# Norm stages of a two-layer encoder: a second unit's low halves placed after the scaling, spare matmuls, split transfers

## The chip, the cores and the metric

One NeuronCore of a Trainium2 chip runs the whole kernel in one launch. The metric is the device time of that core in microseconds (us), the median of several executions; lower is better.

## The reference

The kernel computes two layers of an encoder over 256 tokens of width 1024, all in float32.

```
x = x + mixer(rmsnorm(x, norm_mix[i]))     # layer 0: gated delta net, layer 1: Mamba-2 SSD
x = x + peer(rmsnorm(x, norm_ffn[i]))      # product-key expert retrieval over 128 x 128 experts
...
return rmsnorm(x, norm_final)
rmsnorm(x, w) = x * rsqrt(mean(x * x) + 1e-6) * w
```

Each of the four inner norms stands between two stages of heavy matrix products; a fifth norm makes the output. The change is in these norms, in the loading of x and in the storing of the output.

## The kernel before

**Weights.** All weight matrices come as a stream of *units* of 128x1024 floats (512 KB). SP (SyncE) loads them into `ring`, which has four slots. Every product of the stream is made of three products of rounded parts, hi x hi, lo x hi and hi x lo, so each unit is cut in two halves of 128x512 and each half is split: ScalarE writes the rounded part `w_hi` (L1368, signal `hi_ready`), then GpSimd (L1739) or, in the expert stages, VectorE (L900) writes the rest `w_lo = ring - w_hi` (signal `lo_ready`). Four halves fit in `w_hi` and `w_lo`. TensorE (L359) waits for `lo_ready` of the half it is about to use and raises `half_used`. SP reloads a ring slot when its low halves are made. ScalarE splits two units ahead.

**A norm.** `norm(i)`, i = 0 to 3, has a part on each engine. VectorE adds the products of the last stage to `x_sb` (L908, `x_added`), and ScalarE squares and sums four 128x512 pieces (L1394). VectorE makes the mean (L860), ScalarE its root (L1399), VectorE the factor (L862 to L867). Eight scalings of 128x256 on VectorE (L874) write `h_tok` (an area of `arena`), each raises `n_h`. TensorE's `turn_h` waits for two of them at a time and transposes four 128x128 blocks into a PSUM bank (L379), sixteen in all. ScalarE copies eight 128x256 pieces to `hT_hi` (L1368), VectorE writes the corrections to `hT_lo` (L878), and the first unit's products take them one by one (`await_h`). Each unit of these stages is 24 products of 256 columns into one bank, which ScalarE then copies out (L1368 `arena<-bank`).

**The units around a norm.** The first unit of the next stage is split before the norm. ScalarE splits the second one right after the root, in `norm(i)`, and GpSimd makes its low halves as soon as `hi_ready` allows, since `rest_of_units(..., at[...] + 2)` runs over both units. After the second unit GpSimd issues the load of the expert keys (norms 1 and 3, L1756), or splits the gate weights (norm 2, L1760 and L1762, behind waits for `n_h`, `half_used` and the gates' load).

**The ends.** SP loads x in one transfer of 1 MB (L317), then the first units. ScalarE issues the constants and the norm weights, GpSimd eleven small loads; GpSimd waits for all eleven before it splits the first gate weights and makes its first low half. The last norm multiplies two pieces of 128x1024 (L1361), and SP stores both in one transfer of 1 MB (L352). `Sqrt` on ScalarE needs a function table other than the one loaded first in norm 0; in the later norms a dummy `Sqrt` on `n_idle` loads it ahead of the squares.

**What sets the order.** Every engine's program is written out by hand, and only the named semaphores tie them together; there is no scheduler.

## Time and profile before

| | |
|---|---|
| median of 3 runs | 2238.69 us (2238.45 to 2240.41) |
| profiled execution | 2239.61 us |
| its span, first to last instruction | 2237.8 us |
| mean granted TensorE clock | 0.982 |
| TensorE matmul busy | 2149.9 us (96%) |
| VectorE, ScalarE, GpSimd busy | 1485.1, 1335.9, 1072.2 us |
| norm 0, 1, 2, 3, 4 in the span | 7 to 19, 276 to 290, 1124 to 1137, 1378 to 1392, 2226 to 2234 us |

The profile is of one execution and is read against that execution's own time. Busy TensorE is not TensorE at its peak, since the ends of matmuls are modelled. The granted clock is given as a share of the full 2.4 GHz; 0.5 is 1.2 GHz. A row of the timeline shows the start, the length, the engine, the line, the operation with its target and source, shapes and count, and in brackets how long the engine was idle before it and what released it.

### The profile page before, as it was taken

What the parts mean: (1) busy time and instruction counts of PE and PEld (TensorE: products, weight loads), DVE (VectorE), ACT (ScalarE), POOL (GpSimd) and SP (SyncE); (2) the same over time, 40 slices, a digit from 0 to 9 for tenths busy, and PEclk for the clock granted to TensorE, in tenths of its full rate; (3) what the DMA queues carried; (4) which work ended last, traced back from release to release, by engine and by line L of the source; (5) the groups of instructions that cost most, each with busy time, mean ns of one, the idle gap of its engine ahead of it and who ended that gap; (6) DMA issues with size and microseconds to landing.
All of it is one profiled execution on the core that took longest, in us unless ns stands there. A gap on an engine that the chain in (4) does not pass through costs nothing.

```text
span 2237.8 us, 46017 instructions
## 1 busy us (share of the span) xinstructions
PE 2149.9 (96%) x14384; PEld 1983.2 (89%) x14384; DVE 1485.1 (66%) x3206; ACT 1335.9 (60%) x2736; POOL 1072.2 (48%) x827
## 2 busy tenths in 40 slices
PE   7989799999999999999989988999999999999998
PEld 6979699999999988888889877999999999888886
DVE  5766319994666577777766662299666665777776
ACT  6754355578777644444466765555777885444444
POOL 6841377997766700000056447799976675000000
PEclk9989899999999999999999989999999999999999
DMA  5520254554444566666645225555544445666664
GB/s 169 166 61 1 65 168 146 169 170 158 141 141 140 157 196 193 193 194 190 196 123 161 86 76 169 158 173 161 177 144 138 140 141 173 194 195 190 196 190 148
DMA packets 93872, 343.66 MB, mean 154 GB/s; under 512 B 10688, under 2 KB 10752, under 8 KB 93152
## 3 DMA queue, kind: packets, MB, share of 16 engines
q1 hardware_dynamic: 92592, 338.21, 49.5%
q0 software_dynamic: 912, 4.07, 0.6%
q8 instruction: 47, 0.77, 0.1%
q10 hardware_dynamic: 288, 0.34, 0.0%
q14 instruction: 33, 0.27, 0.0%
HBM read 341.53 MB, written 1.05 MB: 153 GB/s over the span
## 4 chain that ended last, share of the span: by engine, by line
PE 82%; POOL 7%; issue 5%; DVE 3%; ACT 2%; DMA 0%; POOLq 0%; DVEq 0%; ACTq 0%
PE bank L359 80%; POOL w_lo L1739 7%; PE bank L524 0%; ACT w_hi L1368 0%; PE bank L379 0%; DMA small<-in_ssd_d 0%; ACT arena L1394 0%; DVE arena L874 0%; ACT arena L1368 0%; DVE arena L989 0%; DVE arena L1190 0%; DVE arena L1029 0%; DVE arena L996 0%; DVE arena L925 0%; ACT arena L1529 0%
## 5 line engine op out<-in xcount | busy, mean ns | idle before, releaser
L1739 POOL TENSOR_TENSOR w_lo<-ring,w_hi 128x512 fp32r<-128x512 f32 x744 | 994.1, 1350 | 682.9 <-ACT w_hi L1368 670.7
L1368 ACT ACTIVATE w_hi<-ring 128x512 fp32r<-128x512 f32 x1280 | 802.7, 628 | 530.3 <-PE bank L359 527.8
L359 PE MATMUL bank<-hT_hi,w_hi 128*128 128x256 f32 x2688 | 779.8, 290 | 7.9 <-POOL w_lo L1739 6.0
L359 PE MATMUL bank<-hT_lo,w_hi 128*128 128x256 f32 x2688 | 761.0, 283 | 0.0
L359 PE MATMUL bank<-hT_hi,w_lo 128*128 128x256 f32 x2688 | 760.9, 283 | 0.0
L359 PEld LDWEIGHTS bank<-hT_hi,w_hi 128*128 128x128 f32 x2688 | 515.8, 192 | 18.9 <-POOL w_lo L1739 18.4
L359 PEld LDWEIGHTS bank<-hT_lo,w_hi 128*128 128x128 f32 x2688 | 516.4, 192 | 0.0
L359 PEld LDWEIGHTS bank<-hT_hi,w_lo 128*128 128x128 f32 x2688 | 515.5, 192 | 0.0
L900 DVE TENSOR_TENSOR w_lo<-ring,w_hi 128x512 fp32r<-128x512 f32 x536 | 378.2, 706 | 197.3 <-ACT w_hi L1368 189.9
L359 PE MATMUL bank<-w_hi,p_ag_hi 128*128 128x512 f32 x1024 | 398.4, 389 | 0.0
L359 PE MATMUL bank<-w_lo,p_ag_hi 128*128 128x512 f32 x1024 | 398.4, 389 | 0.0
L359 PE MATMUL bank<-w_hi,p_ag_lo 128*128 128x512 f32 x1024 | 398.3, 389 | 0.0
L359 PEld LDWEIGHTS bank<-w_hi,p_ag_lo 128*128 128x128 f32 x1024 | 192.2, 188 | 40.1
L359 PEld LDWEIGHTS bank<-w_hi,p_ag_hi 128*128 128x128 f32 x1024 | 192.2, 188 | 40.0
L359 PEld LDWEIGHTS bank<-w_lo,p_ag_hi 128*128 128x128 f32 x1024 | 192.2, 188 | 39.6
L1283 DVE TENSOR_TENSOR arena<-bank,arena 128x512 f32 (+1 forms) x128 | 88.4, 691 | 166.9 <-PE bank L359 166.9
L359 PE MATMUL bank<-arena 128*128 128x128 f32 (+2 forms) x1072 | 138.0, 283 | 9.4 <-ACT arena L1543 3.2
L359 PEld LDWEIGHTS bank<-arena 128*128 128x128 f32 x1072 | 134.0, 198 | 13.5 <-issue 3.6
L925 DVE SCALAR_TENSOR_TENSOR arena<-bank,small,arena 128x254 f32<-128x254 f32 x192 | 92.5, 482 | 49.1 <-ACT arena L1368 43.7
L1676 ACT ACTIVATE work<-work,small 128x128 f32<-128x128 f32 x256 | 112.8, 488 | 20.2 <-ACT work L1670 19.6
L1326 DVE TENSOR_TENSOR p_ag_lo<-arena,p_ag_hi 128x256 fp32r<-128x256 f32 x256 | 111.0, 433 | 8.9
L1649 ACT ACTIVATE work<-bank 128x256 f32<-128x256 f32 x144 | 55.1, 383 | 84.4 <-PE bank L359 84.4
(241 smaller groups left out, 2244.5 us busy)
## 6 DMA issues: line engine op xcount, KB each, us to landing
ring<-in_peer_u SPq DMA_DIRECT2D x256, 512.0 KB, 3.5
ring<-in_peer_v SPq DMA_DIRECT2D x256, 512.0 KB, 4.1
ring<-in_peer_wq SPq DMA_DIRECT2D x32, 512.0 KB, 3.5
ring<-in_gdn_qkv SPq DMA_DIRECT2D x24, 512.0 KB, 3.5
ring<-in_ssd_xbc SPq DMA_DIRECT2D x24, 512.0 KB, 3.6
ring<-in_ssd_z SPq DMA_DIRECT2D x16, 512.0 KB, 3.5
ring<-in_ssd_out SPq DMA_DIRECT2D x16, 512.0 KB, 3.6
ring<-in_gdn_z SPq DMA_DIRECT2D x8, 512.0 KB, 3.5
```

The costliest lines, as they stand in the source:

```text
L359: return pe.matmul(o, w, r, start=first, stop=last)
L900: dve.tensor_tensor(w_part[1][:, s, :], ring[:, n % RING, hf * 512:(hf + 1) * 512], w_part[0][:, s, :].bitcast(F32), ALU.subtract).then_in ...
L925: ins = dve.scalar_tensor_tensor(o, bank[:, lo + s:hi + s], taps[:, m, j:j + 1], o, ALU.mult, ALU.add)
L1283: dve.tensor_tensor(v, PS[2 + q % 4][:, :].rearrange("p (t i) -> p i t", t=4), v, ALU.mult).then_inc(SEM["p_mul"], 1)
L1326: dve.tensor_tensor(p_ag[1][:, i % 2, :], v, p_ag[0][:, i % 2, :].bitcast(F32), ALU.subtract).then_inc(SEM["p_ag"], 1)
L1368: return act.activation(o, i, ACT.Copy, scale=scale)
L1649: act.activation(p_act[:, i % 2, :], PS[i % 2][:, 0:T], ACT.Gelu).then_inc(SEM["p_gelu"], 1)
L1676: act.activation(row, row, ACT.Relu, bias=p_T[:, 2, tok], scale=p_minus[:, tok]).then_inc(SEM["p_hotS"], 1)
L1739: pool.tensor_tensor(w_part[1][:, s, :], ring[:, n % RING, hf * 512:(hf + 1) * 512], w_part[0][:, s, :].bitcast(F32), ALU.subtract).then_i ...
```

## The change

- **GpSimd.** In norms 1, 2 and 3 only the first unit's low halves are made ahead; before the second unit's, GpSimd waits until all eight scalings are done (`n_h` at 16, 24 and 32). The load of the keys now stands ahead of that wait; the gate split of norm 2 stands behind the second unit as before, without a wait of its own for `n_h`.
- **TensorE.** `turn_h` starts with spare products whose result in bank 3 nobody reads: 18 of `hT_hi` with itself in norms 1 to 3 (128x512, the rounded form), 3 of `ident` with `const` in norm 0 (128x512, plain float32).
- **x.** Two transfers of 512 KB, one for each half of the tokens, with a semaphore each; in norm 0 ScalarE squares the first half's two pieces, then the second's.
- **Root's table.** In norm 0 too a dummy `Sqrt` stands ahead of the squares; VectorE first fills `n_root` with ones for it.
- **The output.** Each half is stored when its own product is done.

```diff
@@ block.sync @@
-            sp.dma_start(x_sb[:, :, :], a["x"]).then_inc(x_loaded, 16)
+            for t in range(NT):
+                sp.dma_start(x_sb[:, t, :], a["x"][:, t, :]).then_inc(x_loaded[t], 16)
...
-            sp.wait_ge(SEM["finished"], 1)
-            sp.dma_start(out, x_sb[:, :, :]).then_inc(SEM["stored"], 16)
-            sp.wait_ge(SEM["stored"], 16)
+            for t in range(NT):
+                sp.wait_ge(SEM["finished"], t + 1)
+                sp.dma_start(out[:, t, :], x_sb[:, t, :]).then_inc(SEM["stored"], 16)
+            sp.wait_ge(SEM["stored"], 16 * NT)
@@ block.tensor, turn_h @@
+                for e in range(KEEP_WARM if i else 3):
+                    if i:
+                        mm(PS[3][:, :], hT[0][:, 0, 0:P], hT[0][:, 0:2, :])
+                    else:
+                        mm(PS[3][:, :], ident, const[:, 0:4, :])
                 for b in range(4):
                     pe.wait_ge(n_h, 8 * i + 2 * (b + 1))
@@ block.vector @@
-            dve.wait_ge(x_loaded, 16)
+            dve.memset(n_root, 1.0).then_inc(root_primed, 1)
+            for t in range(NT):
+                dve.wait_ge(x_loaded[t], 16)
...
-                ins = dve.scalar_tensor_tensor(x_sb[:, t, :], ..., last_gain, ALU.mult, ALU.mult)
-            ins.then_inc(SEM["finished"], 1)
+                dve.scalar_tensor_tensor(x_sb[:, t, :], ..., last_gain, ALU.mult, ALU.mult
+                                         ).then_inc(SEM["finished"], 1)
@@ block.scalar, norm_squares @@
-                if i:
-                    act.activation(n_idle, n_root, ACT.Sqrt)
-                for hf in range(2):
-                    for t in range(NT):
-                        if i:
-                            act.wait_ge(x_added, 4 * (i - 1) + 2 * hf + t + 1)
-                        part = 2 * hf + t
+                if not i:
+                    act.wait_ge(root_primed, 1)
+                act.activation(n_idle, n_root, ACT.Sqrt)
+                for part in range(4):
+                    hf, t = divmod(part, 2) if i else (part % 2, part // 2)
+                    if i:
+                        act.wait_ge(x_added, 4 * (i - 1) + part + 1)
+                    else:
+                        act.wait_ge(x_loaded[t], 16)
@@ block.gpsimd @@
-                rest_of_units(start + 2, tables[lyr] + 2)
+                pool.wait_ge(n_h, 16 * (lyr + 1))
+                rest_of_units(start + 1, tables[lyr] + 2)
...
-            rest_of_units(at[("go", 2)], at[("pq", 0, 0)] + 2)
+            rest_of_units(at[("go", 2)], at[("pq", 0, 0)] + 1)
             load_keys(0)
...
-            rest_of_units(at[("sx", 0)], at[("sx", 2)])
+            rest_of_units(at[("sx", 0)], at[("sx", 1)])
+            pool.wait_ge(n_h, 24)
+            rest_of_units(at[("sx", 1)], at[("sx", 2)])
             pool.wait_ge(s_wg_loaded, 16)
             pool.wait_ge(half_used, 2 * at[("sx", 0)])
-            pool.wait_ge(n_h, 24)
```

The second layer's `rest_of_units(at[("so", 2)], ...)` changes in the same way. How this moves instructions, engine by engine:

GpSimd around norm 1 (after the mixer's last piece of work on `arena`), before: the low halves `w_lo` of both units, the load of the keys, then the low halves of the routing stage up to the loop of the experts.

```order
L1782 TENSOR_TENSOR arena<-arena,work 128x1024 [waits g_zs] x2
L1739 TENSOR_TENSOR w_lo<-ring,w_hi 128x512 [waits hi_ready] x16
L1756 DMA arena<-in_peer_kT 128x2048 [waits x_added]
L1739 TENSOR_TENSOR w_lo<-ring,w_hi 128x512 [waits hi_ready] x32
L1749 UNCONDITIONAL_BRANCH
```

The same place now.

```order
L1793 TENSOR_TENSOR arena<-arena,work 128x1024 [waits g_zs] x2
L1749 TENSOR_TENSOR w_lo<-ring,w_hi 128x512 [waits hi_ready] x14
L1767 DMA arena<-in_peer_kT 128x2048 [waits x_added]
L1749 TENSOR_TENSOR w_lo<-ring,w_hi 128x512 [waits hi_ready,n_h]
L1749 TENSOR_TENSOR w_lo<-ring,w_hi 128x512 [waits hi_ready] x33
L1760 UNCONDITIONAL_BRANCH
```

Two low halves moved behind the load of the keys, and the first of them waits for the scalings as well; norm 3 has the same.

TensorE around norm 1, before: the last products of the delta net's output, then the transposes of `turn_h` (names: `bank` is PSUM, `arena` holds `h_tok`, `const` the identity).

```order
L359 MATMUL bank<-w_hi,hT_hi 128x512
L359 MATMUL bank<-w_lo,hT_hi 128x512
L359 MATMUL bank<-w_hi,hT_lo 128x512
L379 MATMUL bank<-const,arena 128x128 [waits n_h]
L379 MATMUL bank<-const,arena 128x128 x3
```

The same place now.

```order
L363 MATMUL bank<-w_hi,hT_hi 128x512
L363 MATMUL bank<-w_lo,hT_hi 128x512
L363 MATMUL bank<-w_hi,hT_lo 128x512
L363 MATMUL bank<-hT_hi 128x512 x18
L388 MATMUL bank<-const,arena 128x128 [waits n_h]
L388 MATMUL bank<-const,arena 128x128 x3
```

Eighteen products without a wait stand between the stage's last product and the transposes.

ScalarE at the start of the program, before: the loads, a table load, the squares of x, and a second table load ahead of the root.

```order
L1702 DMA small<-in_norms 128x32
L1394 ACT_TABLE_LOAD
L1394 ACTIVATE arena,small<-x_sb 128x512 [waits x_loaded]
L1394 ACTIVATE arena,small<-x_sb 128x512
L1394 ACTIVATE arena,small<-x_sb 128x512 [waits n_squares] x2
L1399 ACT_TABLE_LOAD [waits n_mean]
L1399 ACTIVATE small<-small 128x2 [waits n_squares]
```

The same place now.

```order
L1712 DMA small<-in_norms 128x32
L1399 ACT_TABLE_LOAD
L1399 ACTIVATE small<-small 128x2 [waits root_primed]
L1406 ACTIVATE arena,small<-x_sb 128x512 [waits x0_loaded] x2
L1406 ACTIVATE arena,small<-x_sb 128x512 [waits x1_loaded,n_squares] x2
L1411 ACTIVATE small<-small 128x2 [waits n_mean,n_squares]
```

One table load of two is left, ahead of the squares, and the first two squares wait for the first half of x alone.

## Rows read from the trace of the kernel before

**Rows 1.** The page's chain that ended last, shares of the span by engine.
```profile
PE 82%; POOL 7%; issue 5%; DVE 3%; ACT 2%; DMA 0%; POOLq 0%; DVEq 0%; ACTq 0%
```

**Rows 2.** Timeline of norm 1: start, length, engine, line, operation, idle before.
```profile
276.04 0.39 PE L359 MATMUL bank<-w_lo,hT_hi 128*128 128x512 f32 x1
...
276.95 0.39 PE L359 MATMUL bank<-w_hi,hT_lo 128*128 128x512 f32 x1
...
280.58 2.53 POOL L1739 TENSOR_TENSOR w_lo<-ring,w_hi 128x512 fp32r<-128x512 f32 x2 [3.69 <-ACT w_hi L1368]
280.67 4.16 DVE L874 TENSOR_SCALAR arena<-x_sb,small 128x256 f32<-128x256 f32 x8
...
283.31 3.68 PE L379 MATMUL bank<-const,arena 128*128 128x128 f32 x16 [5.98 <-DVE arena L874]
284.47 3.40 ACT L1368 ACTIVATE hT_hi<-bank,small 128x256 fp32r<-128x256 f32 x8 [3.45 <-PE bank L379]
285.34 3.43 DVE L878 SCALAR_TENSOR_TENSOR hT_lo<-bank,small,hT_hi 128x256 fp32r<-128x256 f32 x8 [0.51 <-ACT hT_hi L1368]
```

**Rows 3.** Timeline of the start and of norm 0.
```profile
1.19 0.46 ACTq L1702 DMA_DIRECT2D small<-in_norms  x1
...
12.27 2.19 DVE L874 TENSOR_SCALAR arena<-x_sb,small 128x256 f32<-128x256 f32 x8
...
13.03 3.65 PE L379 MATMUL bank<-const,arena 128*128 128x128 f32 x16 [13.03 <-DVE arena L874]
...
14.77 3.00 ACT L1368 ACTIVATE hT_hi<-bank,small 128x256 fp32r<-128x256 f32 x8
15.62 3.22 DVE L878 SCALAR_TENSOR_TENSOR hT_lo<-bank,small,hT_hi 128x256 fp32r<-128x256 f32 x8 [1.17 <-ACT hT_hi L1368]
```

**Rows 4.** DMA issues: KB each, median us from issue to landing.
```profile
small<-in_norms ACTq DMA_DIRECT2D x1, 16.0 KB, 9.2
```

**Rows 5.** Chain of waits in order of time: start, length, what.
```profile
6.70 9.29 DMA small<-in_ssd_d
...
18.52 12.98 PE bank L359 x96
...
161.64 1.86 PE bank L359 x16
...
1134.66 11.36 PE bank L359 x96
```

**Rows 6.** TensorE by half microseconds, norms 1, 2: length, busy, granted clock, DMA, GB/s.
```profile
281.00:281.50 0.50, 0.00 (x0) 0.54 0.00 0
...
1134.00:1134.50 0.50, 0.50 (x5) 0.62 0.04 16
```

**Rows 7.** Timeline of ScalarE: the first unit's result read, norms 1, 2 and 3.
```profile
290.33 0.38 ACT L1368 ACTIVATE arena<-bank 128x256 f32<-128x256 f32 x1 [0.74 <-PE bank L359]
...
1137.57 0.47 ACT L1368 ACTIVATE arena<-bank,small 128x256 f32<-128x256 f32 x1 [0.75 <-PE bank L359]
...
1392.66 0.38 ACT L1368 ACTIVATE arena<-bank 128x256 f32<-128x256 f32 x1 [0.75 <-PE bank L359]
```

**Rows 8.** Timeline of norms 2 and 3: scalings, transposes of norm 2, its first product.
```profile
1128.48 4.16 DVE L874 TENSOR_SCALAR arena<-x_sb,small 128x256 f32<-128x256 f32 x8
...
1131.13 3.53 PE L379 MATMUL bank<-const,arena 128*128 128x128 f32 x16 [5.98 <-DVE arena L874]
1134.41 0.36 PE L359 MATMUL bank<-hT_hi,w_hi 128*128 128x256 f32 x1
...
1382.84 4.16 DVE L874 TENSOR_SCALAR arena<-x_sb,small 128x256 f32<-128x256 f32 x8
```

**Rows 9.** The end: SP's store in the timeline, and DMA issues with time to landing.
```profile
2233.54 0.35 SPq L352 DMA_DIRECT2D out<-x_sb  x1
...
ring<-in_peer_u SPq DMA_DIRECT2D x256, 512.0 KB, 3.5
...
out<-x_sb SPq DMA_DIRECT2D x1, 1024.0 KB, 3.9
```

More of the change, by code:

```diff
@@ L64 @@
 EARLY = 56
+KEEP_WARM = 18
 EXP_AT, TURN_AT = 36, 48
@@ L286, in hybrid_encoder @@
         mask = flat(p_ag[1][:, :, :], "s t")
-        x_loaded, small_loaded, gain_loaded = sem("x_loaded"), sem("small_loaded"), sem("gain_loaded")
+        x_loaded, small_loaded, gain_loaded = [sem(f"x{t}_loaded") for t in range(NT)], sem("small_loaded"), sem("gain_loaded")
+        root_primed = sem("root_primed")
         const_loaded = sem("const_loaded")
@@ L1360, in _ @@
             for t in range(NT):
-                ins = dve.scalar_tensor_tensor(x_sb[:, t, :], x_sb[:, t, :], n_rstd[:, t:t + 1], last_gain, ALU.mult, ALU.mult)
-            ins.then_inc(SEM["finished"], 1)
+                dve.scalar_tensor_tensor(x_sb[:, t, :], x_sb[:, t, :], n_rstd[:, t:t + 1], last_gain, ALU.mult, ALU.mult
+                                         ).then_inc(SEM["finished"], 1)
         @block.scalar
@@ L1385, in norm_squares @@
             def norm_squares(i):
-                if i:
-                    act.activation(n_idle, n_root, ACT.Sqrt)
-                for hf in range(2):
-                    for t in range(NT):
-                        if i:
-                            act.wait_ge(x_added, 4 * (i - 1) + 2 * hf + t + 1)
-                        part = 2 * hf + t
-                        act.activation(h_junk[:, (part % 2) * 512:(part % 2 + 1) * 512], x_sb[:, t, hf * 512:(hf + 1) * 512], ACT.Square,
-                                       scale=D ** -0.5, accum_out=n_ss[:, hf, t:t + 1]).then_inc(n_sq, 1)
-                        if part >= 1:
-                            act.wait_ge(n_sq, 4 * i + part)
+                if not i:
[7 more added lines that the diff above has]
+                        act.wait_ge(x_loaded[t], 16)
+                    act.activation(h_junk[:, (part % 2) * 512:(part % 2 + 1) * 512], x_sb[:, t, hf * 512:(hf + 1) * 512], ACT.Square,
+                                   scale=D ** -0.5, accum_out=n_ss[:, hf, t:t + 1]).then_inc(n_sq, 1)
+                    if part >= 1:
+                        act.wait_ge(n_sq, 4 * i + part)
                 act.wait_ge(n_mean, i + 1)
@@ L1401, in norm @@
             def norm(i):
-                if i == 0:
-                    act.wait_ge(x_loaded, 16)
                 norm_squares(i)
@@ L1822, in _ @@
             pool.wait_ge(lo_ready, 2 * at[("so", 2)])
-            rest_of_units(at[("so", 2)], at[("pq", 1, 0)] + 2)
+            rest_of_units(at[("so", 2)], at[("pq", 1, 0)] + 1)
             load_keys(1)
```

## The prediction

> **What bounds the kernel now.** Read first the chain of work that ended last: TensorE holds 82% of the span and GpSimd 7% [rows 1]. Inside the stages TensorE has no gap worth a term, so only the joints matter, above all the five norms, where TensorE has nothing to multiply. Second, read the timeline of norm 1 [rows 2]. The last product of the mixer starts at 276.95. VectorE adds it to x, ScalarE squares, VectorE makes the factor, and the scaling starts at 280.67, while GpSimd subtracts the two low halves of a second unit from 280.58. Eight scalings take 4.16 us there and 2.19 us in norm 0, where GpSimd is idle [rows 3]; that is the cost of the overlap. The transposes start at 283.31, 2.64 us after the scaling; in norm 0 it is 0.76 us (12.27 to 13.03). Third, norm 0: its transposes end at 16.68, but the products start only at 18.52, because the chain there runs through the last small transfer, which lands at 15.99, and then through GpSimd [rows 3, 5]. Fourth, the granted clock: TensorE stops at 277.34, the granted clock falls to half at 281.04 (0.54 is the mean of the half microsecond in which it falls). In norm 2 it comes back at 1134.38 [rows 6]. So the transposes, and in norms 1 and 3 the first products too, run at 1.2 GHz.
>
> **The change, part by part.** The sum is made against the profiled execution: 2239.6 us, of which the span is 2237.8; the median of the runs is 2238.7, 0.9 us below it, and I subtract the same sum from that.
>
> *GpSimd's wait.* With the second unit's two subtractions behind the eighth scaling, the scalings cost 2.19 us instead of 4.16, and what TensorE waits for, the first two of them, is ready 0.76 us after the start: 281.43 instead of 283.31, so 1.88 us earlier. Norms 2 and 3 have the same 4.16 us [rows 8], so their transposes move to 1129.24 and 1383.60. Together 5.6 us. What stands behind the wait on GpSimd: the second unit (2.53 us, now done at 280.67 + 2.19 + 2.53 = 285.4), in norm 2 also the gate split, and every later low half. SP's loads of the next ring slots follow them. TensorE wants the second unit at 286.5 (below), so 1.1 us of cover are left; if it were gone, each missing us would be paid once per norm. The load of the keys is now issued ahead of the second unit instead of behind it; nobody needs the keys before the routing projections end, 45 us later. Cost nothing.
>
> *18 spare products.* They are 128x512 products of the fp32r form whose pace is (276.95 - 276.04) / 4 = 0.2275 us [rows 2]. They start at 277.18 and take 4.10 us: the last start leaves TensorE free at 281.28, 0.15 us before 281.43. The same holds in norms 2 and 3, where the distance from the last product to the scaling is the same. So they delay nothing, and TensorE is never idle while the clock would fall. What the high clock gives: the transposes go from 0.23 us (3.68 / 16) to an estimated 0.114 us each. The first four then end after 0.46 us; ScalarE follows 0.25 us later as now (1.16 - 0.91), VectorE 0.85 us after it as in norm 0 (14.77 to 15.62), and its eight corrections take 3.22 us [rows 2, 3]. Three products at 11.36 / 96 = 0.118 us and the tail of the last one make 0.6 us. So the first unit is done 0.46 + 0.25 + 0.85 + 3.22 + 0.6 = 5.4 us after the first transpose, and VectorE, no longer TensorE, sets this piece. ScalarE reads the first unit's result now at 290.33, 1137.57 and 1392.66 [rows 7]; by this sum at 286.8, 1134.6 and 1389.0. Gains 3.5, 3.0 and 3.7, together **10.2 us**, of which 5.6 is GpSimd's wait and 4.6 the clock. From there on every wait in the trace is on another engine's work, none on a fixed time, so the whole shift should reach the end.
>
> *The start.* The second table load goes, and x in two transfers lets half the squares run earlier. Price: nothing, because the cover is the small transfer that lands at 15.99 and the 2.5 us that GpSimd needs behind it, up to 18.52. But three spare products stand ahead of the transposes and wait for the norm weights, which land at 1.19 + 9.2 = 10.4 [rows 3, 4]. Their form, plain float32 with 512 columns, does not occur before. The nearest row has eight such products of 128 columns in 1.86 us at the full clock [rows 5], 0.23 each; four times the columns are 0.93, and 1.86 at half the clock. Lower bound 3 x 0.93 = 2.8 us, upper 5.6 us; I take 5 us, since they start at the low clock. Then the transposes run from about 15.4 to 17.5 and the corrections end near 20.3, in time for the second half unit, whose low half comes at about 19.7. The products start at 18.5 as now. If the clock is high then, the first 96 products take as long as in norm 2: 11.36 us from 1134.66, and 0.25 us because the first started at 1134.41 [rows 5, 8]. Now they take 12.98: **1.4 us**. Bounds: 1.4 gained, 0 if the clock falls in the pause before 18.5, and 0.8 lost if it stays low throughout and the transposes end at 19.3. I take 1.4: the pause would be some 1 us, and in norm 1 the clock held 3.7 us after TensorE stopped.
>
> *The output.* The first half leaves 1.2 us before the second; the second starts when the whole one does now, at 2233.54. The whole one, 1 MB, lands in 3.9 us, and transfers of 512 KB in 3.5 us [rows 9]. So **0.4 us**, bounds 0 and 1.
>
> *Sum:* 10.2 + 1.4 + 0.4 = 12.0 us. 2239.6 - 12.0 = 2227.6; on the median 2238.7 - 12.0 = **2226.7 us**.
>
> **Two rules against the rows.** In norm 2 the clock rose at 1134.38, when TensorE had done nothing but transposes since 1131.13 (its first product starts at 1134.41) [rows 6, 8]. The Trainium skill, "TensorE: Matmul & The Clock Gate", section "Part 4: PE-mode transpose", says that transposes do not count as work for the clock. By that rule the clock could fall during the transposes of every norm, and the sum would be near that of rival B; this row speaks against it, though in norm 0 3.65 us of transposes raised nothing. On the output: the Trainium skill, "DMA: Bandwidth & Descriptors", section "Anatomy of one DMA", puts a transfer at 2 us plus its bytes at 436 GB/s. By that, an estimate, half the size is 1.2 us shorter and the sum 12.8; no run here shows it yet.
>
> **The rivals.**
> *A, the clock is low at 18.5.* Norm 0 before had transposes until 16.68, a pause of 1.84 us, and low-clock products until 21.5. If the spare products leave the clock low, or it falls in the pause, the start gives 0: 2238.7 - 10.6 = 2228.1. For it: the pause is there still. Against: five us of dense work ahead of it.
> *B, the spare products don't hold the clock.* The transposes come 1.88 us earlier and everything after them runs as slowly as now: 5.6 + 0.4, so 2232.7. For it: between transposes and corrections TensorE waits on VectorE for short stretches, and the rule above. Against: the granted clock stayed full for 3.7 us of complete idleness in norm 1, and these pauses are tenths of a us.
> *C, slower.* The spare products run at half the pace because the clock is already low when they start: 18 x 0.455 = 8.2 us, the transposes wait until 285.4 instead of 283.31, 2.1 us late three times, and the start loses 0.8: 2238.7 + 6.3 + 0.8 - 0.4 = 2245.4. It decides from the point where the 18 take over 6.1 us (283.31 - 277.18), a pace of 0.34. The row at 276.95 still has the full pace and the fall comes at 281.04, so little speaks for it.
> *D, the joint is bound elsewhere.* The earlier start meets another late thing: GpSimd's chain of low halves (1.1 us of cover) or a ring slot loaded late. If it takes 2.5 of the 3.4 us in each norm, 2.7 + 0.4 are left: 2235.6, no measurable change. GpSimd needs 2.53 / 2 = 1.27 us for a half [rows 2], TensorE 12 x 0.118 = 1.42, so a lag is worked off; nothing else in the rows is that near.
>
> **How the numbers follow.** Chances: the forecast 0.50, A 0.28, B 0.12, D 0.07, C 0.03. The likeliest is 2226.7. The range starts at 2224.7 (the output at its upper bound, and 1.4 us for clock falls elsewhere that may land otherwise once everything is shifted) and ends at 2232.8, which takes in A and B and leaves out C and D, 1 in 10, beside the little below the low end. A measurement of this kernel tells about 0.2%, 4.5 us, from no change, so faster means below 2234.2: the forecast, A and B, 0.90. Same is D, 0.07; slower is C, 0.03.
>
> **What would show it.** In the profile after: the eight scalings at 2.2 us in norms 1 to 3, none of them above 0.4 us; 18 products of 128x512 at 0.23 us ending within 0.2 us of the first transpose; a granted clock of 1.00 from the last product of the mixer to the second unit; the corrections starting 1.5 us after the first transpose; ScalarE's first copy 3.0 to 3.7 us earlier relative to the mixer's last product. At the start, products at 0.12 us from 18.5. I am wrong if TensorE idles ahead of the second unit on GpSimd's low half, if the spare products end after the second scaling, or if the shift of 10 us is there at 1400 and not at the end.

## The result and the profile after

The changed kernel takes **2224.8 us** (median of 4 runs, 2222.63 to 2225.72) against 2238.8 us before (median of 4 runs beside it, 2238.45 to 2240.41): a ratio of 0.9934, 95% interval [0.992, 0.9949]. That is 14.0 us less, where 12.0 were forecast: faster as forecast, and by 2 us more. The median lies 0.1 us inside the low end of the range, 2224.7; but the ratio, applied to the 2238.7 us that the prediction counts from, gives 2223.9 and lies below it. The profiled execution took 2225.72 us, its span is 2223.9 us (2237.8 before).

The chain that ended last has the same shape as in [rows 1]; nothing new has become the bound:

```profile
PE 82%; POOL 7%; issue 5%; DVE 2%; ACT 2%; DMA 1%; POOLq 0%; DVEq 0%; ACTq 0%
```

Norm 1 after, in the timeline (start, length, engine, line, operation, idle before). It answers to [rows 2]:

```profile
277.95 4.24 PE L363 MATMUL bank<-hT_hi 128*128 128x512 f32 x18
...
279.74 0.58 POOL L1767 DMA_DIRECT2D arena<-in_peer_kT  x1 [2.31 <-DVE x_sb L917]
...
281.46 2.19 DVE L883 TENSOR_SCALAR arena<-x_sb,small 128x256 f32<-128x256 f32 x8
282.13 1.99 PEld L388 LDWEIGHTS bank<-const,arena 128*128 128x128 f32 x16 [0.36 <-DVE arena L883]
282.13 2.23 PE L388 MATMUL bank<-const,arena 128*128 128x128 f32 x16
282.83 3.03 ACT L1379 ACTIVATE hT_hi<-bank,small 128x256 fp32r<-128x256 f32 x8 [1.02 <-PE bank L388]
283.70 3.23 DVE L887 SCALAR_TENSOR_TENSOR hT_lo<-bank,small,hT_hi 128x256 fp32r<-128x256 f32 x8
283.74 2.53 POOL L1749 TENSOR_TENSOR w_lo<-ring,w_hi 128x512 fp32r<-128x512 f32 x2 [3.42 <-DVE arena L883]
...
287.64 0.39 ACT L1379 ACTIVATE arena<-bank 128x256 f32<-128x256 f32 x1 [0.88 <-PE bank L363]
```

The eight scalings take 2.19 us instead of 4.16, GpSimd's second unit stands behind them, the 18 spare products fill TensorE's wait to within 0.36 us of the first transpose, and the transposes start 0.67 us after the scaling instead of 2.64. From the scaling's start to ScalarE's first copy it is 287.64 - 281.46 = 6.18 us; before it was 290.33 - 280.67 = 9.66 [rows 2, 7]. The granted clock stays at 1.00, that is 2.4 GHz, where it was 0.54 and 0.62 in [rows 6] (length, busy TensorE, its weight loads, VectorE, ScalarE, GpSimd, granted clock, DMA share, GB/s):

```profile
281.00:281.50 0.50, 0.50 (x4) 0.42 (x3) 0.40 (x4) 0.50 (x2) 0.00 (x0) 1.00 2.05 262
...
1134.00:1134.50 0.50, 0.50 (x6) 0.50 (x6) 0.46 (x2) 0.11 (x1) 0.50 (x1) 1.00 0.00 0
```

The start, the timeline of TensorE and then the chain of waits [rows 3, 5]:

```profile
8.86 4.48 PE L363 MATMUL bank<-const 128*128 128x512 f32 x6 [8.86 <-DMA small<-in_norms]
13.17 1.91 PE L388 MATMUL bank<-const,arena 128*128 128x128 f32 x16
19.00 0.58 PE L363 MATMUL bank<-hT_hi,w_hi 128*128 128x256 f32 x1 [3.92 <-POOL w_lo L1749]
```

```profile
6.69 9.78 DMA small<-in_ssd_d
...
19.00 13.14 PE bank L363 x96
```

A plain float32 product shows as two records, so x6 are the three spare ones: 4.48 us. The transposes run at the high clock, then TensorE waits 3.92 us for GpSimd's low half, and the granted clock falls just as the products start:

```profile
18.50:19.00 0.50, 0.00 (x0) 0.00 (x0) 0.50 (x2) 0.50 (x3) 0.50 (x2) 1.00 0.00 0
19.00:19.50 0.50, 0.50 (x2) 0.50 (x3) 0.50 (x2) 0.50 (x2) 0.50 (x1) 0.51 0.00 0
...
22.00:22.50 0.50, 0.50 (x4) 0.50 (x4) 0.00 (x0) 0.45 (x1) 0.50 (x1) 0.57 0.82 336
```

The output: two stores of 512 KB, each landing in 2.7 us, instead of one of 1 MB in 3.9 [rows 9].

```profile
out<-x_sb SPq DMA_DIRECT2D x2, 512.0 KB, 2.7
```

**Where the time went.** I cut both spans at the start of the scaling in each norm, at the end of the first 96 products, at the start of the last product before TensorE's first long pause in the second layer's mixer, and at the first product of the last norm. The mixer pieces of one trace are not the kernel's own lengths, as the experiments will show. The last column is a second profiled run of the changed kernel (`e10_changed_again`, below). All in us.

| piece | forecast | before | after | difference | after, second run |
|---|---|---|---|---|---|
| to the end of the first 96 products | -1.4 | 31.50 | 32.14 | +0.64 | +0.15 |
| rest of the first layer's mixer, to norm 1 | 0 | 249.17 | 249.32 | +0.15 | -2.76 |
| norm 1 and the experts | -3.5 | 847.81 | 844.34 | -3.47 | -3.48 |
| norm 2 and projections, to the pause | -3.0 | 85.48 | 82.56 | -2.92 | -2.92 |
| rest of the second mixer, to norm 3 | 0 | 168.88 | 165.24 | -3.64 | -0.05 |
| norm 3 and the experts | -3.7 | 848.19 | 844.69 | -3.50 | -3.64 |
| last norm and output | -0.4 | 6.8 | 5.7 | -1.1 | -1.1 |
| span | -12.0 | 2237.8 | 2223.9 | -13.9 | -13.8 |

So the norms gave nearly what was forecast (9.9 of 10.2), the start did not bring its 1.4 us, the output gave nearly three times its 0.4, and 3 us came in the mixers, which the change doesn't touch. The experiments take these one by one.

### The profile page after: what moved, and what is told of

It is laid out like the page before. It is cut to its first block, busy times and chain, and to the rows that moved or that the text cites. A ratio compares the mean times of both kernels' runs of the same rounds, so it can differ in the third digit from the quotient of the medians.

```text
span 2223.9 us, 46144 instructions
## 1 busy us (share of the span) xinstructions
PE 2156.1 (97%) x14444; PEld 1984.6 (89%) x14444; DVE 1479.7 (67%) x3207; ACT 1334.2 (60%) x2736; POOL 1072.7 (48%) x827
## 3 DMA queue, kind: packets, MB, share of 16 engines
HBM read 341.53 MB, written 1.05 MB: 154 GB/s over the span
## 4 chain that ended last, share of the span: by engine, by line
PE 82%; POOL 7%; issue 5%; DVE 2%; ACT 2%; DMA 1%; POOLq 0%; DVEq 0%; ACTq 0%
PE bank L363 81%; POOL w_lo L1749 7%; PE bank L533 1%; ACT w_hi L1379 0%; DMA small<-in_ssd_d 0%; ACT arena L1379 0%; PE bank L388 0%; DVE arena L998 0%; DVE arena L1199 0%; DVE arena L1038 0%; DVE arena L1005 0%; DVE arena L934 0%; ACT arena L1539 0%; PE bank L457 0%; POOL small L1742 0%
## 5 line engine op out<-in xcount | busy, mean ns | idle before, releaser
L363 PEld LDWEIGHTS bank<-hT_hi,w_hi 128*128 128x128 f32 x2688 | 515.1, 192 | 21.5 <-POOL w_lo L1749 20.3
L363 PEld LDWEIGHTS bank<-arena 128*128 128x128 f32 x1072 | 132.0, 196 | 13.7 <-issue 3.6
L1686 ACT ACTIVATE work<-work,small 128x128 f32<-128x128 f32 x256 | 112.7, 487 | 20.2 <-ACT work L1680 19.6
```

The lines of the kernel that those rows point to most:

```text
L363: return pe.matmul(o, w, r, start=first, stop=last)
L1686: act.activation(row, row, ACT.Relu, bias=p_T[:, 2, tok], scale=p_minus[:, tok]).then_inc(SEM["p_hotS"], 1)
```

## The experiments

**The two parts of the norms, each alone.** First GpSimd's order, in the kernel before:

```
-                rest_of_units(start + 2, tables[lyr] + 2)
+                pool.wait_ge(n_h, 16 * (lyr + 1))
+                rest_of_units(start + 1, tables[lyr] + 2)
```

(and the same order in norm 2.)

> The kernel before with GpSimd's wait alone. The theory of the prediction: the eight scalings of norms 1 to 3 fall from 4.16 to 2.2 us, the first transpose comes 1.88 us earlier in each, and nothing else changes, so 5.6 us less than before, 0.9975. Rival, the clock in the second layer's mixer: between the scalings of norm 2 and norm 3 the changed kernel was 6.56 us shorter where 3.0 was forecast, and its granted clock was low for 6.8 us there instead of 20.5. If those low stretches depend only on where a pause of TensorE happens to fall in time, this kernel too may have another number of them, and that interval may be shorter or longer by some 3.4 us than the 1.9 that the shift explains.

Measured: 2229.49 us (5 runs, 2227.97 to 2230.8), ratio 0.9958 [0.9944, 0.9972], 9.3 us less. The theory had 5.6 us and 1.9 per norm. The intervals of norms 1 and 3 are 845.39 and 845.57, that is 2.42 and 2.62 us shorter, and the piece of norm 2 is 1.79 shorter, 6.8 together. The rest of this trace's gain lies in the mixers, as in the changed kernel. In its timeline of norm 1 the transposes start 0.67 us after the scaling and still take 3.55 us:

```profile
279.62 2.19 DVE L874 TENSOR_SCALAR arena<-x_sb,small 128x256 f32<-128x256 f32 x8
...
280.29 3.55 PE L379 MATMUL bank<-const,arena 128*128 128x128 f32 x16 [4.01 <-DVE arena L874]
```

The clock falls there too, at 280.5, just behind a pause of 4.01 us (before it fell inside one of 5.98 [rows 2]), but it is low for 3.4 us instead of 6.8, and so it is in norms 2 and 3. The shorter wait came with a shorter low stretch, a gain that I had booked under the spare products.

Then the 18 spare products alone:

```
             def turn_h(i):
+                for e in range(18 if i else 0):
+                    mm(PS[3][:, :], hT[0][:, 0, 0:P], hT[0][:, 0:2, :])
```

> The kernel before with the 18 spare products in norms 1 to 3 alone. The theory of the prediction: the spare products end 2.0 us before the transposes can start at 283.3, the clock stays high through that short pause, and the first unit is done 5.4 us after the first transpose: 4.6 us less than before, 0.9979. Rival: the pause of 2 us lets the clock fall in some norms, and then those gain nothing: 0 to 4.6 us. As in the first run, the low stretches between the scalings of norms 2 and 3 may add or take 3.4 us.

Measured: 2237.33 us (11 runs, 2233.4 to 2239.76), ratio 0.999 [0.9981, 0.9999]. The theory had 4.6 us less; the rival, that the norms gain nothing, came nearly true. The intervals behind norms 1 and 3 are 847.44 and 848.03: 0.4 and 0.2 us shorter; the piece of norm 2 is no shorter. With GpSimd in the way of the scalings the 18 products end 1.92 us ahead of the first transpose; the clock is still high when the transposes start and falls within them:

```profile
280.91 2.69 PE L381 MATMUL bank<-const,arena 128*128 128x128 f32 x16 [1.92 <-DVE arena L876]
```

```profile
281.00:282.00 1.00, 1.00 (x9) 0.79 (x9) 1.00 (x5) 0.40 (x2) 0.24 (x1) 1.00 0.67 61
282.00:283.00 1.00, 1.00 (x8) 0.89 (x8) 0.95 (x4) 1.00 (x4) 0.00 (x0) 0.73 0.56 209
283.00:284.00 1.00, 1.00 (x6) 1.00 (x5) 1.00 (x3) 1.00 (x4) 0.00 (x0) 0.50 1.09 451
```

Either the pause that is left makes it fall, or the transposes don't hold it. To tell these apart, the same kernel with 27 instead of 18, which reach the first transpose:

> The kernel before, GpSimd's order untouched, with 27 instead of 18 spare products ahead of the transposes of norms 1 to 3: 6.14 us, which reaches from 277.18 to 283.32, where the transposes start in that kernel. With 18 (the run of the spare products alone) the two norm intervals were only 0.4 and 0.2 us shorter than before, since a pause of 2 us remained and the clock fell in it. Theory (the pause is what lets the clock fall): no low-clock stretch after norms 1 to 3, the intervals behind norms 1 and 3 are 1.5 to 2 us shorter than before (845.8 to 846.3 and 846.2 to 846.7), time 2232.5 to 2234.5 us. Rival (the transposes do not hold the clock, filled pause or not): the intervals stay within 0.5 us of before, time 2237 to 2238.

Measured: 2230.87 us (5 runs, 2229.41 to 2232.28), ratio 0.9965 [0.9951, 0.9978]. No low stretch behind norms 1, 2 and 3, as the theory said; the intervals behind norms 1 and 3 are 846.39 and 846.56, 1.42 and 1.63 us shorter (the first just short of the theory's range), and the piece of norm 2 is 84.57 instead of 85.48, 0.9 shorter. The time is 1.6 us better than the theory's range; in the trace the second mixer takes 165.3 us where it took 168.88 before. Its norm 1:

```profile
276.01 6.28 PE L359 MATMUL bank<-hT_hi 128*128 128x512 f32 x27
...
282.21 2.00 PEld L381 LDWEIGHTS bank<-const,arena 128*128 128x128 f32 x16 [0.35 <-DVE arena L876]
282.22 2.23 PE L381 MATMUL bank<-const,arena 128*128 128x128 f32 x16
```

So filling the pause decides, and these transposes, between spare products and products, ran at the high clock throughout. That speaks against the rule that I weighed (the Trainium skill, "TensorE: Matmul & The Clock Gate", "Part 4: PE-mode transpose": transposes do not count as work for the clock) as a rival for this kernel, without deciding the rule itself: 16 of them last only 2.2 us here. The two parts together: GpSimd's wait alone gives 2.4 us in norm 1, the clock alone (27 products) 1.4, both 3.5. The clock is worth some 1.0 us per norm on top of GpSimd's wait (1.05, 1.13 and 0.88 in norms 1, 2 and 3), not 1.5; the forecast's 10.2 us was nearly right in sum and wrong in its split.

**The output alone**, the two stores and nothing else:

```
-            sp.wait_ge(SEM["finished"], 1)
-            sp.dma_start(out, x_sb[:, :, :]).then_inc(SEM["stored"], 16)
+            for t in range(NT):
+                sp.wait_ge(SEM["finished"], t + 1)
+                sp.dma_start(out[:, t, :], x_sb[:, t, :]).then_inc(SEM["stored"], 16)
...
```

(VectorE raises `finished` after each half.)

> The kernel before with the output alone in two transfers. By the prediction 0.4 us less; by the changed kernel's trace, where the end of the span came 5.6 us after the start of the last product instead of 6.8, 1.2 us less. In the trace the time from the first product of 128x1024 to the end of the span decides: 6.4 or 5.6 us, whatever the rest of the run does.

Measured: 2237.22 us (11 runs), ratio 0.9995 [0.9986, 1.0004]; the time alone can't tell it from none, but the end of the span can: from the last norm's first product to the end it is 1.1 us shorter, in this trace as in those of the changed kernel. The Trainium skill, "DMA: Bandwidth & Descriptors", section "Anatomy of one DMA", leads to an estimate of 1.2 us for half the bytes. The traces agree with that difference (3.9 to 2.7 us) but not with the whole times, which by it, again estimates, would be 4.4 and 3.2; the page's fit is for transfers that GpSimd issues, and these are issued by SP. My rows for 512 KB, 3.5 us, were loads issued in the middle of the kernel, and the store runs alone; that this is the reason for the difference was not tested.

**The start.** First the changed kernel without its three spare products in norm 0 (`range(KEEP_WARM if i else 3)` becomes `range(KEEP_WARM if i else 0)`):

> The changed kernel without the three spare products of norm 0. If they bring nothing, since the clock falls again in the pause before the first unit (granted 0.51 from 19.0 us), the first unit starts at the same time and at the same clock, and the time is the changed kernel's within 0.3 us. If they cost something, the transposes would now start at about 12.1 instead of 13.2, and the first product earlier than 19.0; but that one waits for GpSimd, which waits for the last small load, so I expect 0. Between the scalings of norm 2 and norm 3 this kernel is the changed one: 247.8 us again if its low stretches are fixed by the program, another value if they are not.

Measured: 2225.83 us (5 runs, 2220.89 to 2227.57), ratio 0.9936 [0.9923, 0.995]: no difference to the changed kernel that can be told. Its first 96 products are in the chain of waits:

```profile
18.32 14.26 PE bank L363 x96
```

They take 14.26 us; before they took 12.98 [rows 5]. The transposes now start at 11.92 instead of 13.03, the pause behind them is 2.75 us instead of 1.84, and the products run longer at the low pace (0.21 us each until beyond 23 us, before until 21.5). But this is no price of the earlier norm, for the start of before has the same spread: `e1_pool_only` and `e8_27_spare`, whose programs up to norm 1's scaling are that of before, show

```profile
18.67 14.16 PE bank L359 x96
```

```profile
18.59 14.14 PE bank L359 x96
```

and `e2_spare_only` and `e3_output_only`, with that same start, take 13.11 us each: there the clock was up at 16.2 and 16.4 and fell at 19.6 and 19.8, behind a pause of 2.0 us. With the three spare products it is 13.14, 13.11 and 13.12 us in three traces, without them 12.98 to 14.26 in six. The 96 products end at 31.50 to 32.84 us, in the mean 32.08, in the five traces with the start of before, and at 31.64 to 32.14, in the mean 31.89, in three of the changed kernel's start. So the start gained about 0.2 us, and what it was to bring went into the pause. The two transfers of x and the root's table were not run alone; norm 0's scaling starts at 11.0 to 11.3 us with them and at 12.2 to 12.4 without.

If the pause of 3.9 us is what costs it, filling it must give it back. Four more such products behind the transposes of norm 0:

```
                     last.then_inc(n_hTps, 1)
+                for e in range(0 if i else 4):
+                    mm(PS[3][:, :], ident, const[:, 0:4, :])
```

> The changed kernel, with four more plain float32 128x512 spare products behind norm 0's transposes. In the changed kernel TensorE ends those transposes near 15.1 us, waits 3.9 us, the granted clock falls at 19.0 just as the first product starts, and the first 96 products take 13.14 us instead of some 11.6. Theory (the fall comes from the pause): four spare products of about 0.87 us fill 15.1 to 18.6, the clock stays full, the first 96 products take 11.6 to 11.8 us, and the scaling of norm 1 starts 1.4 us earlier than in the changed kernel, at 280.1 instead of 281.5: time 2223.4 us. Rival (the start is bound by low halves of weights, the clock only hides behind them): the 96 products still take 13 us and the time stays at 2224.8. Second rival (more work ahead only brings the fall sooner): the clock is low already at 19.0 and the time is 2225 to 2226.

Measured: 2223.07 us (5 runs, 2220.16 to 2225.38), ratio 0.9934 [0.992, 0.9947]. In the profiled run the clock is 1.00 from 15 to 23 us (its first recorded change is at 13.5):

```profile
15.63 3.60 PE L363 MATMUL bank<-const 128*128 128x512 f32 x8
18.66 0.68 PE L363 MATMUL bank<-hT_hi,w_hi 128*128 128x256 f32 x1
19.18 0.28 PE L363 MATMUL bank<-hT_lo,w_hi 128*128 128x256 f32 x1
```

```profile
19.00:20.00 1.00, 1.00 (x9) 0.94 (x8) 1.00 (x4) 0.26 (x1) 1.00 (x2) 1.00 0.00 0
```

The first 96 products run from 18.66 to 30.58, 11.9 us with their start, and end 1.56 us earlier than in the changed kernel. The theory held for the start: the 1.4 us of the forecast were there, behind a pause that my sum had put at 1 us and that is 3.9. In `e7_all_warm` and `e9_all_warm_2`, which have the same bridge, the 96 products end at 30.88 and 30.37; the mean of the three is 1.3 us ahead of the mean of the unfilled ones. Norm 1's scaling starts at 276.00 instead of the expected 280.1, because this run also lacks two falls in the first mixer. The median is 1.7 us below that of the changed kernel, but the runs of the two overlap.

**The 3 us in the mixers.** Ahead of the second layer's pause at 1214 before and 1208 after, nothing differs but the norm. At its end, before and after (same columns as above):

```profile
1216.00:1218.00 2.00, 0.59 (x1) 0.50 (x2) 0.78 (x2) 1.13 (x2) 0.95 (x2) 0.57 0.54 164
1218.00:1220.00 2.00, 2.00 (x6) 1.64 (x5) 0.77 (x3) 0.97 (x2) 0.21 (x1) 0.50 0.75 281
```

```profile
1210.00:1212.00 2.00, 0.18 (x1) 0.18 (x2) 1.15 (x3) 0.79 (x3) 1.02 (x1) 1.00 0.54 219
1212.00:1214.00 2.00, 1.81 (x8) 1.25 (x8) 0.58 (x3) 1.37 (x2) 0.55 (x1) 1.00 0.90 299
```

In both TensorE waits 3.18 us for ScalarE. Before, the clock is low from 1216.3 to 1223.1, all but the first 1.1 us of it under products; after, it doesn't fall. At the next pause (6.02 us in both, 1321.5 before, 1313.9 after) it is low for 13.7 us before and for 6.8 after, all of these 6.8 inside the wait and the transposes. The first piece is 2.01 us longer before (103.67 against 101.66 from pause to pause), the second 1.63 (65.21 against 63.58, from there to norm 3's scaling). To see whether these are the clock, I filled both pauses of the changed kernel:

```
+                pe.wait_ge(SEM["s_cumsb"], 1)
+                for e in range(14):
+                    mm(PS[3][:, :], hT[0][:, 0, 0:P], hT[0][:, 0:2, :])
                 pe.wait_ge(SEM["s_silued"], SC)
...
                 y_head(SH - 1)
+                for e in range(26):
+                    mm(PS[3][:, :], hT[0][:, 0, 0:P], hT[0][:, 0:2, :])
```

> The changed kernel, with 14 spare 128x512 fp32r products in TensorE's pause at 1208.4 us and 26 in its pause at 1313.9 us, both in the second layer's mixer. Theory (the 3.6 us that the mixer of the second layer gained beyond the sum are clock falls that landed otherwise): the interval from norm 2's scaling to norm 3's is 247.8 us or a little less (246.5 to 247.8), with none of it at the low clock, in every run; in the run of the changed kernel without spare products at the start it was 251.5 with 20.5 us at the low clock. Rival (the mixer is shorter because something else moved): the interval stays where the clock's state does not reach it, near 249 to 250. If the 26 run into the transposes at 1319.9 they cost up to 0.3 us. Time 2223.5 to 2224.8 us.

Measured: 2225.51 us (5 runs, 2222.59 to 2225.85), 0.7 us above the expected range and no faster than the changed kernel. The interval is 247.84 with no low stretch in it: the 247.80 of the changed kernel's profiled run was already the floor, and its 6.8 us at the low clock cost nothing there. In e4_no_spare_at_start, the same program from norm 1 on, the same interval is 251.49 with 20.5 us at the low clock. So these microseconds are the clock's, and where it falls seems not to be fixed by the program. The changed kernel itself once more:

> The changed kernel itself, to see how far its clock falls differ from run to run. Theory (where the clock falls in the pauses of the mixers is not fixed by the program): median 2223.5 to 2225.5 us, runs spread over 3 us or more, and in the profiled run at least one of the falls at 19, 118, 230 and 1316 us is missing or longer. Rival (the program fixes them): the same falls within 1 us, intervals between the norms within 0.2 us of the profiled run of the changed kernel (270.12, 844.34, 247.80, 844.69).

Measured: 2225.02 us (5 runs, 2223.79 to 2226.44), ratio 0.9936 [0.9923, 0.995]. The same program, and its profiled run has other falls:

| at the low clock | first mixer, us | second mixer, us |
|---|---|---|
| before | 3.4 at 117, 10.2 at 147, 3.4 at 229, 13.7 at 243 | 6.8 at 1216, 13.7 at 1322 |
| after, first profiled run | 3.4 at 118, 10.2 at 148, 3.4 at 230, 13.7 at 244 | none, 6.8 at 1316 |
| after, second profiled run | none, 10.2 at 145, none, 13.7 at 241 | 6.8 at 1207, 13.7 at 1313 |

```profile
1207.00:1209.00 2.00, 0.60 (x2) 0.51 (x3) 0.77 (x2) 1.14 (x2) 0.96 (x2) 0.55 0.55 176
1209.00:1211.00 2.00, 2.00 (x6) 1.64 (x5) 0.78 (x3) 0.96 (x2) 0.20 (x1) 0.50 0.90 291
```

The theory held, but for the spread, which is 2.7 us. In this run the second mixer takes as long as before (168.83 against 168.88) and the first is 2.8 us shorter instead. The second mixer without costly falls takes 165.2 us (e5_bridge, e6_ssd_warm and the first run agree within 0.1), the first 245.4 or less (e5_bridge, 276.00 - 30.58).

That shorter first mixer is no gain of the change. Only three of these traces have the falls at 118 and 230, before, after and e6_ssd_warm, and their first mixer takes 249.2 to 249.3 us; in six others it takes 246.4 to 246.9, and four of these six are kernels whose first mixer is that of before (246.69 in e3_output_only). The profiled run of before was one with long falls there. The second mixer is another matter. With the norms of before it takes 168.88 and, in e3_output_only, 169.01 us; with GpSimd's wait alone 166.7, with 18 spare products alone 166.0, with 27 165.3, and with both parts 165.24, 168.83, 168.94 (e4_no_spare_at_start) and 165.24 (e5_bridge). The mean granted clock, known for every run, agrees: 0.981 to 0.985 in the 40 runs of before beside the experiments, 0.987 to 0.991 in the nine of the changed kernel. As time at the low clock this is 78 us against 50 in the mean, and of the 28 us of difference the three norms explain 20.5 (three stretches of 6.8).

**All pauses.** Last, spare products in the long pauses of TensorE in both mixers: e5_bridge and e6_ssd_warm together, and in the first mixer

```
+                pe.wait_ge(SEM["g_P"], GH - 1)
+                for e in range(20):
+                    mm(PS[2][:, :], hT[0][:, 0, 0:P], hT[0][:, 0:2, :])
                 for n in range(GB, LEVELS * GB + 2):
...
                 pe.wait_ge(SEM["g_int"], 4)
+                for e in range(9):
+                    mm(PS[4][:, :], hT[0][:, 0, 0:P], hT[0][:, 0:2, :])
                 pe.wait_ge(SEM["g_vn1"], 4)
...
                 for t in range(NT):
+                    pe.wait_ge(SEM["g_O"], 3 * t + 1)
+                    for e in range(24 if t else 14):
+                        mm(PS[4 + 2 * t][:, :], hT[0][:, 0, 0:P], hT[0][:, 0:2, :])
                     pe.wait_ge(o_ready, t + 1)
```

> The changed kernel with the additions of the two kernels before it, and spare products in four more pauses of the first layer's mixer: 20 at 146 us, 9 at 228 us, 14 at 240 us, 24 at 245 us. In the changed kernel 30.8 us between norm 0 and norm 1 run at the low clock outside the start. Theory (each fall follows a pause, and filling the pauses holds the clock): at most 10 us at the low clock are left there, that interval shrinks by 3 to 7 us, since part of the low-clock stretches is bound by VectorE anyway, and the time is 2217 to 2221 us. Rival (the mixer's joints are bound by VectorE and ScalarE): the clock holds but the interval shrinks by less than 1.5 us, time 2222 to 2223.5. Second rival (the spare products start at a low clock, take twice as long and end behind the data they bridge to): slower, 2226 to 2230.

Measured: **2219.31 us** (4 runs, 2217.29 to 2220.54), ratio 0.991 [0.9895, 0.9926], faster than both kernels. 6.8 us at the low clock are left in the interval, which is 264.80 instead of 270.12. But e5_bridge has 264.96 with 20.5 us at the low clock, at 146 and 238: they cost at most some tenths of a us there, while those at 118 and 230, which it lacks as six other traces do, make 2.5 us. TensorE is busy for 4.2 us of the 6.8 from 146.6 and for 6.0 of the 13.7 from 238.8, so waits fill much of these stretches; which engine bounds them was not traced. One of the falls that stay comes after the pause, under products that follow each other without a gap:

```profile
249.00:250.00 1.00, 1.00 (x5) 0.78 (x6) 0.00 (x0) 0.00 (x0) 0.00 (x0) 0.92 0.00 0
250.00:251.00 1.00, 1.00 (x4) 0.81 (x3) 0.00 (x0) 0.00 (x0) 0.00 (x0) 0.50 0.00 0
```

TensorE had waited 2.55 us until 248.86 there. And with spare products between the back-transposes too, ahead of the fall at 116:

```
+                    if gi == 0:
+                        pe.wait_ge(SEM["g_cumsb"], 1)
+                    for e in range(0 if gi % 2 else 4 if gi else 2):
+                        mm(PS[3][:, :], hT[0][:, 0, 0:P], hT[0][:, 0:2, :])
                     pe.wait_ge(SEM["g_qk"], gi // 2 + 1)
```

> The kernel with all pauses filled, and also 14 spare products of 0.23 us between the pairs of back-transposes from 112 us on, where TensorE waits 1.1 us twice and where the granted clock fell at 116 in the kernel with all pauses filled. Theory (each fall follows pauses): that fall is gone, the two falls that stay (3.4 us each, at 249 and 1307 us) follow pauses that cannot be filled, because the operand of the spare products is being rewritten there; time 2217 to 2219 us. Rival (the fall at 116 lies under work that VectorE bounds): the fall goes, the time stays at 2219.3.

Measured: 2219.75 us (4 runs, 2219.73 to 2220.09), ratio 0.9914 [0.9899, 0.9929]. The fall at 116 is gone, two of 3.4 us stay, at 248 and 1306. The rival held as to the time, which is that of the kernel before it, just above the theory's range; that VectorE is what bounds there was not shown. Its four runs lie within 0.4 us, where those of the changed kernel spread over 3.1 and 2.7.

## Why the prediction was off

Two steps failed. The pause ahead of norm 0's first product was put at "some 1 us" and was 3.9, so the start brought about 0.2 us instead of 1.4. And falls of the clock in the mixers were given no term in the sum and 1.4 us in the range, where they made about 3 us; this is the step that carried the result past the forecast. The output was mis-sized, 0.4 instead of 1.1.

*The norms, forecast 10.2 us:* nearly right in size (3.47, 2.92, 3.50, together 9.9) and in its steps: 18 spare products at 0.23 us, the first transpose 0.36 us behind the last of them (0.15 expected), transposes of 0.114 us expected and 2.23 us for sixteen, the corrections 1.57 us after the first transpose (1.5 expected), the fall gone. The cover that D doubted held: TensorE never waits for the second unit. B and C are excluded: TensorE's clock held, and the spare products had the full pace. The split between wait and clock was wrong, since the shorter wait also came with a shorter low stretch (e1_pool_only), and the two help each other: 18 products only bridge the wait because GpSimd no longer lengthens it (e2_spare_only, e8_27_spare).

*The start, forecast 1.4 us gained:* this is the first step that failed, the pause before 18.5. The terms behind it: the norm weights landed at 8.9 instead of the 10.4 I took from [rows 4], where the pair of issue and landing of before had been read as fixed (the runs don't show why it came sooner); the three products took 4.5 us instead of 5; and the transposes ran at the high clock, in 1.9 us. So they ended at 15.1 and not at 17.5, and the pause became 3.9 us. Being earlier made the pause longer, and the clock fell as the products began: the end of the 96th product is 0.64 us later, of which 0.5 is the last small transfer (9.78 us to land instead of 9.29; in the second run 9.31, and the end 0.15 later). That is the mechanism of rival A, given a chance of 0.28; it had read the pause of before, 1.84 us, as a reason. Rightly: in e2_spare_only and e3_output_only, with the start of before, the clock fell behind a pause of 2.0 us while in norm 1 it had held for 3.7 us of idleness, the row that I leaned on. e5_bridge shows what the pause costs: filled, it gives 1.56 us against the first profiled run. The bound on the loss was also added up wrong: 10.4 + 5.6 + 3.65 is 19.65, so 1.1 us and not 0.8.

*The output, forecast 0.4 us:* mis-sized; it measured 1.1, a little above the upper bound of 1. The row of loads in the middle of the kernel was the wrong neighbour for a store that runs alone, and the estimate by the Trainium skill, "DMA: Bandwidth & Descriptors", section "Anatomy of one DMA", which I had kept out of the sum, was near for the difference.

*The mixers, no term:* the range held 1.4 us "for clock falls elsewhere that may land otherwise". They were worth about 3. The trace of before had the falls at 1216 and 1322, with products under them: 2.0 and 1.6 us that could go. I didn't read them because the change doesn't touch these lines. Where the clock falls depends on the run: the changed kernel's second mixer was short in its first profiled run and as long as before in its second, and e2_spare_only's runs fall into a group of five near 2234, mean granted clock 0.988, and a group of six near 2238.5, clock 0.985. But with the norms of before the second mixer was long in both traces, and none of 40 runs of before had a granted clock above 0.985. Why before should carry the costly falls of the second mixer more often than the kernels with shorter or warmer norms is **not settled**; that the stages start at other times is a guess, and no run shifts them alone.

With the sum as it should have been, norms 9.9, output 1.1, start 0.2, 11.2 us are measured piece by piece. The other 2.8 of the 14.0 are put down to falls of the clock elsewhere: the traces show their size in the second mixer, and not why their mean changed. That the total came within 2 us of the forecast is in part luck: the start's missing 1.2 us and the mixers' 3 had opposite signs.

## What to carry to other kernels

When spare products are to hold the clock, first make the wait short and fixed, then size them so that they reach the next real product: with 2 us left open they gave 0 to 0.4 us per norm, with none left 0.9 to 1.6. Making an early stage faster lengthens the pause behind it if something else (here a small transfer) fixes the next start; work that ends earlier needs a longer bridge. Before a change is priced, list every stretch of the trace below the full clock and ask which of them lie under TensorE's own work: they come and go from run to run, and their sum (here some 7 us: 1.3 at the start, 2.5 and 3.6 in the mixers) is the width that a range needs. One profiled run of the kernel before can be an unusual one: compare pieces with several traces that share the same program up to that point.

## What the runs showed of the hardware

- A fall of the clock can come after the pause: at 19.0 in the changed kernel, as the first product starts, after 3.92 us of waiting; in e2_spare_only 1.6 us after the transposes began, after a pause of 1.92 us; in e7_all_warm about 1 us after the products began.
- The same program has different falls in different executions, with the second mixer 3.6 us longer or shorter for it (251.39 and 247.80 us from norm 2 to norm 3), while the total of two runs was the same within 0.1 us (2225.72 and 2225.76).
- Ahead of the first recorded change of the clock the granted clock reads 1.00 whatever the pace: in the kernel before it is 1.00 from 15 to 22 us, where transposes take 0.23 us and products of 256 columns 0.21, twice their pace later. At the very start the pace of the products has to be read, not that column; the tables above count only falls that the column shows.
- A plain float32 product with 512 columns takes about 0.86 to 0.9 us at the high clock (four products, eight records, in 3.60 us in e5_bridge), against 0.23 us for the rounded form.
